# Another opening for a macaron layer: conditioning with the weights held still, spread through the first round

## What is computed

```
ada = (silu(c) @ w_ada + b_ada).reshape(B, N_MOD, D_MODEL)
xn = _modulate(_rms(x, g_ffn1), ada[:, 0], ada[:, 1])
x = x + 0.5 * ada[:, 2][:, None] * _swiglu(xn, w_ffn1_gate, w_ffn1_up, w_ffn1_down)
xn = _modulate(_rms(x, g_mix), ada[:, 3], ada[:, 4])
m, new_buf, h_last, v_state = _mixer(xn, ...)
x = x + ada[:, 5][:, None] * m
xn = _modulate(_rms(x, g_ffn2), ada[:, 6], ada[:, 7])
x = x + 0.5 * ada[:, 8][:, None] * _swiglu(xn, w_ffn2_gate, w_ffn2_up, w_ffn2_down)
```

## Time and profile before

| what | us |
| --- | --- |
| median of 3 runs | 2510.47 (2510.26 to 2513.07) |
| profiled execution | 2516.07 |
| span in its trace | 2514.3 |
| TensorE busy | 2411.8 (96%) |
| VectorE busy | 1672.5 (67%) |
| ScalarE busy | 1053.6 (42%) |
| GpSimd busy | 148.2 (6%) |

### The profile page before, as it was taken

One profiled execution on the slowest core, in us unless ns is written; L12 is line 12 of the kernel. 1 busy time (PEld: TensorE's weight loads), 2 busy tenths in 40 slices (PEclk: granted clock), 3 DMA queues, 4 the chain that ended last, 5 costly groups with the idle time before them and its releaser, 6 DMA issues.

```text
span 2514.3 us, 31914 instructions
## 1 busy us (share of the span) xinstructions
PE 2411.8 (96%) x11469; PEld 2030.0 (81%) x11469; DVE 1672.5 (67%) x2660; ACT 1053.6 (42%) x1825; POOL 148.2 (6%) x186
## 2 busy tenths in 40 slices
PE   7889999999999999999999999988999999999997
PEld 3567777777788877999999999986777788878886
DVE  4976767766666685666666666469677667656666
ACT  3454444444333353433344434135444444433334
POOL 3000000000000000000111110000000000000000
PEclk9999999999999999999999999989999999999998
DMA  9244554455976333312222123413544543497642
GB/s 359 72 159 151 176 176 150 151 177 184 346 263 226 134 126 104 127 54 63 63 63 61 56 59 98 152 55 117 175 149 151 174 147 123 151 353 278 226 134 78
DMA packets 245521, 381.03 MB, mean 152 GB/s; under 512 B 16658, under 2 KB 158154, under 8 KB 243991
## 3 DMA queue, kind: packets, MB, share of 16 engines
q1 hardware_dynamic: 232702, 345.15, 39.6%
q0 software_dynamic: 10240, 33.56, 4.9%
q10 hardware_dynamic: 2456, 0.75, 0.1%
HBM read 262.93 MB, written 116.47 MB: 151 GB/s over the span
## 4 chain that ended last, share of the span: by engine, by line
PE 71%; DVE 15%; DMA 5%; issue 4%; ACT 3%; SPq 1%; DVEq 0%; ACTq 0%
PE bank L512 21%; PE bank L513 20%; PE bank L514 20%; DMA h_dram<-stage_lo 3%; DVE u_lo L604 3%; PE bank L2800 2%; PE bank L2802 2%; PE bank L2803 2%; DMA wraw<-in_w_ffn_down 1%; DVE stage_lo L1932 1%; DVE wraw L631 1%; DVE ada_lo L1947 1%; PE bank L2818 1%; DVE h L1940 1%; DVE x L2110 1%
## 5 line engine op out<-in xcount | busy, mean ns | idle before, releaser
L604 DVE TENSOR_TENSOR u_lo<-wraw,u_hi 128x512 fp32r<-128x512 f32 (+2 forms) x532 | 317.4, 618 | 285.6 <-ACT u_hi L598 282.8
L512 PE MATMUL bank<-ops,u_hi 128*128 128x512 f32 x1232 | 488.5, 397 | 13.5 <-ACT g L1201 10.5
L513 PE MATMUL bank<-ops,u_hi 128*128 128x512 f32 x1232 | 485.3, 394 | 0.0
L514 PE MATMUL bank<-ops,u_lo 128*128 128x512 f32 x1232 | 484.2, 393 | 0.0
L598 ACT ACTIVATE u_hi<-wraw 128x512 fp32r<-128x512 f32 (+2 forms) x532 | 289.2, 567 | 267.3 <-PE bank L514 167.6
L512 PE MATMUL bank<-xn_hi,w_hi 128*128 128x384 f32 x1104 | 370.1, 335 | 6.2 <-ACT ww L1606 2.0
L514 PE MATMUL bank<-xn_hi,w_lo 128*128 128x384 f32 x1104 | 368.8, 334 | 0.0
L513 PE MATMUL bank<-xn_lo,w_hi 128*128 128x384 f32 x1104 | 368.8, 334 | 0.0
L512 PEld LDWEIGHTS bank<-ops,u_hi 128*128 128x128 f32 x1232 | 234.3, 190 | 77.4 <-ACT g L1201 11.3
L514 PEld LDWEIGHTS bank<-ops,u_lo 128*128 128x128 f32 x1232 | 233.8, 190 | 50.8
L513 PEld LDWEIGHTS bank<-ops,u_hi 128*128 128x128 f32 x1232 | 234.4, 190 | 49.1
(11 more groups left out here) (321 smaller groups left out, 4257.3 us busy)
## 6 DMA issues: line engine op xcount, KB each, us to landing
h_dram<-stage_hi SPq DMA_DIRECT2D x154, 256.0 KB, 2.4
h_dram<-stage_lo SPq DMA_DIRECT2D x154, 256.0 KB, 2.7
ada_raw<-in_w_ada POOLq DMA_DIRECT2D x96, 256.0 KB, 3.0
raw<-in_w_in SPq DMA_DIRECT2D x48, 512.0 KB, 4.7
wraw<-in_w_ffn_gate SPq DMA_DIRECT2D x44, 512.0 KB, 3.9
wraw<-in_w_ffn_up SPq DMA_DIRECT2D x44, 512.0 KB, 4.9
wraw<-in_w_ffn_down SPq DMA_DIRECT2D x48, 384.0 KB, 4.7
x<-x_dram SPq DMA_DIRECT2D x6, 2304.0 KB, 12.0
```

The lines of the kernel that those rows point to most:

```text
L512: nc.tensor.matmul(out, hi, mov_hi, start=first, stop=False, skip_group_check=True)
L513: nc.tensor.matmul(out, hi, mov_lo, start=False, stop=False, skip_group_check=True)
L514: return nc.tensor.matmul(out, lo, mov_hi, start=False, stop=last, skip_group_check=True)
L604: nc.vector.tensor_tensor(unit(u_lo, f, g, u, n), unit_source(u, n), unit(u_hi, f, g, u, n).bitcast(F32), ALU.subtract).then_inc(u_lo_read ...
```

## The change

**The conditioning products.** In `first_half` the sides are exchanged: blocks of 128x128 of the conditioning weights are stationary and the 9 columns of `cT` move, 32 matmuls a half. The result comes out turned, so the row copies (`first_rows`) and their transposes (`first_turn`) go, and VectorE adds the bias from the bank.

```diff
-FIRST_HALVES = [(v, half) for v in (SCALE1, SHIFT1, GATE1) for half in range(2)]
+FIRST_HALVES = [(SCALE1, 0), (SHIFT1, 0), (SCALE1, 1), (SHIFT1, 1), (GATE1, 0), (GATE1, 1)]
+FIRST_BANKS = (7, 6, 7, 2, 7, 7)
...
-                for k in range(KT):
-                    last = nc.tensor.matmul(bank[(3, 4, 3, 4, 7, 2)[n]][0:NSEQ, :], cT[:, k, 0:NSEQ], w_ada_sb[:, n, k, :],
-                                            start=k == 0, stop=k == KT - 1)
+                for b in range(4):
+                    o = b * NSEQ
+                    for k in range(KT):
+                        last = nc.tensor.matmul(bank[FIRST_BANKS[n]][:, o:o + NSEQ], w_ada_sb[:, n, k, b * P:(b + 1) * P],
+                                                cT[:, k, 0:NSEQ], start=k == 0, stop=k == KT - 1,
+                                                skip_group_check=True)
```

```diff
-            pe.wait_ge(rows_copied, 2)
+            pe.wait_ge(rows_copied, 1)
+            x_turn(2)
+            first_half(0)
             pe.wait_ge(x_in, 2 * NT)
-            first_half(0)
+            for c in range(3):
+                spread(0, c)
             first_half(1)
...
+                    prompt(0, A11[1], O_B11, X[1], True, False,
+                           between=(lambda: spread(2, 1)) if f == 1 else None)
+                    if f == 0:
+                        first_half(2)
+                        pe.wait_ge(xs_lo_ready, 1)
+                    else:
+                        pe.wait_ge(xs_lo_ready, 3)
                     samples_in(0, 0)
                     if f == 0:
-                        first_turn(4)
-                        first_turn(5)
-                        pe.wait_ge(ada_ready, 6)
+                        first_half(3)
...
                     prompt(0, S2[1], O_T2, X[1], False, False)
+                    if f == 0:
+                        first_half(4)
                     pe.wait_ge(snapped, snaps(f, 0, 3))
                     prompt(0, S3[0], O_T3, X[0], False, False, True)
                     pe.wait_ge(snapped, snaps(f, 0, 4))
                     prompt(0, S3[1], O_T3, X[1], False, False)
+                    if f == 0:
+                        first_half(5)
```

```diff
+            def row_squares(lo, hi):
+                for t in range(lo, hi):
+                    act.wait_ge(x_loaded[t // 3], 32 if t >= 6 else 16)
+                    if t > 1:
+                        act.wait_ge(sumsq_mm, t - 1)
+                    nc.scalar.activation(spent[:, t % 2, :], xrow[:, t, :], ACT.Square, accum_out=nrst[:, t:t + 1])\
+                      .then_inc(sumsq_mm, 1)
```

```diff
-            sp.wait_ge(x_loaded[1], 16)
             ada_half(0)
             ada_half(1)
-            first_weights(0)
+            weights(0, 0, 0, 0)
+            weights(0, 0, 1, 0)
+            sp.wait_ge(x_in, 8)
+            spill(slice(0, KH), x_spilled, slice(0, PH))
             ada_half(2)
             ada_half(3)
...
+            weights(0, 0, 0, 1)
+            weights(0, 0, 1, 1)
+            sp.wait_ge(x_spilled, 16)
+            spill(slice(KH, KT), x_spilled, slice(0, PH))
             sp.wait_ge(rg_loaded, 64)
...
+            sp.wait_ge(x_in, 2 * NT)
+            spill(slice(0, KH), x_spilled_late, slice(PH, TOK))
+            sp.wait_ge(sumsq_mm, 9)
+            ada_half(4)
+            sp.wait_ge(x_spilled_late, 16)
+            spill(slice(KH, KT), x_spilled_late, slice(PH, TOK))
```

```diff
             def sample_operand(f):
...
-                    samples_modulated(0, xs, xs, xs)
-                for k in range(KH):
-                    op_scale(f, k, 1)
+                    for k in range(KH):
+                        op_scale(f, k, 1)
                 dve.wait_ge(samples_act, FACTORS_MADE["hi", f])
...
+                if f == 1:
+                    for k in range(KH):
+                        op_scale(f, k, 1)
```

```diff
-                for o in range(2):
-                    slot_ = wslot(U_OUT + o)
-                    rows = slice(k * P, (k + 1) * P)
-                    for c in range(NCH):
+                rows = slice(k * P, (k + 1) * P)
+                for c in range(NCH):
+                    for o in range(2):
+                        slot_ = wslot(U_OUT + o)
...
-            last.then_inc(out_mm, 6)
+                        if k == KT - 1:
+                            last.then_inc(out_mm, 1)
```

More of the change, by code:

```diff
@@ L114 @@
                                (1, 4, True), (1, 6, True)]
-SQUARES = ([(c, k, False) for c in range(2) for k in range(KT)],
+SQUARES = ([],
            FFN1_SQUARES,
@@ L150, in added, with squares_done, summed_squares, sample_steps @@
 def added(i, pos):
-    return sum(is_added(j, q) for j in range(i) for q in range(NSQ)) + sum(is_added(i, q) for q in range(pos))
+    return sum(is_added(j, q) for j in range(1, i) for q in range(NSQ)) + sum(is_added(i, q) for q in range(pos))
+def squares_done(i, pos):
+    return NSQ * (i - 1) + pos + 1
+def summed_squares(i, c):
+    return (4, 8, 9)[c] if i == 0 else 9 + 3 * (i - 1) + RANK[i][c]
+def sample_steps(i):
+    return 3 * i + 3 if i > 0 else 0
 def ring_use(i, pos):
@@ L529, in made @@
     def made(f, g, u):
+        if f == 0 and isinstance(g, int) and g == 0:
+            return u + 1
         return g * 16 + (f * ALL * 16 + MADE[u] + 1)
@@ L1168, in first_units @@
             def first_units(f):
-                for u in EARLY:
+                for u in (EARLY if f == 1 else range(4)):
                     unit_hi(act, f, 0, u)
@@ L1175, in op_hi @@
                 v_shift = norm_scales(i)[0]
[L1176 removed]
+                if f == 0 and o in (O_B11, O_B21):
+                    act.wait_ge(ada_ready, 2 if o == O_B11 else 4)
+                elif f == 0 and o == O_T3:
                     act.wait_ge(ada_mm, 5)
@@ L1542, in _ @@
                     act.dma_start(rg_sb[64 * h:64 * h + 64, :, g, 64 * h:64 * h + 64], src).then_inc(rg_loaded, 16)
[L1544 to L1555 removed]
+            for c in range(3):
+                factor_copy(0, c)
             first_units(0)
@@ L2775, in units_ready, with prompt @@
                     pe.wait_ge(u_lo_ready, made(f, g, u))
-                def prompt(g, u, o, out, first, last_, staged=False):
+                def prompt(g, u, o, out, first, last_, staged=False, between=None):
                     units_ready(g, u)
@@ L2786, in prompt @@
                                        first and k == 0, last_ and k == KH - 1)
+                        if between is not None and k == 1:
+                            between()
                     last.then_inc(ffn_mm, 1)
```

351 lines of the change are left out of this document (153 added, 198 removed).

## The result

The changed kernel takes 2536.26 us (median of 4 runs, 2532.91 to 2539.12) against 2510.36 us before: a ratio of 1.0099, with a 95% interval of 1.0087 to 1.0112. The forecast was 2520, with a range up to 2529. The direction was right, the size was not: 25.9 us instead of 9.5. The profiled execution took 2532.91 us. With the six further runs of the first experiment (median 2535.12) and 29 of the kernel before beside them (median 2511.64, single executions from 2505.47 to 2518.86) the difference is 23.5 us. The two profiled executions lie only 17 us apart, since that of before was a slow one of its kind (2516.07) and that of after a quick one.

A forecast was written before the change was run, and what follows sets the result against it. TensorE, busy 96% of the span, was taken as the bound, with the opening read at VectorE's first join. Opening +17.0, FFN2 -6.8 and output projection -0.9 gave +9.3 us over the 2510.47 median: 2520 us, range 2497 to 2529.

The forecast's parts named there:

- The forecast's first step: Conditioning products: narrow passes halve the clock without a TensorE gap, a pass going from 0.106 to 0.204 us.
- rival 1: Conditioning products: the clock holds through narrow passes, 6.8 us a half, join at 121.4, time 2495 us; chance 0.22.
- The queue: Opening: late transfers make VectorE wait up to 5 us more, 2525 to 2530; chance 0.12 together with more halves at half clock.
- The waits behind halves 4 and 5: Round 0: half 4 holds ScalarE and VectorE by overwriting the place of T3's operand; TensorE then idles 3.6 us.
- the price of half 0: Start of the opening: 10.3 us from 23.19, the clock falling 3 us in; FFN1 then starts at 50.0.
- when S2 starts: Round 0 of FFN1: S2 follows T2's first low tile at 102.0 us; its 24 products end at 107.5.
- nothing between the opening and FFN2: After TensorE's wait on ada_lo at 161.57 us: no gap that matters, so no term for later rounds of FFN1.
- nothing changes between the join and the wait on ada_lo: VectorE from 129.53 to 161.57 us: same work before and after, its only long pause 3.75 us for stage-buffer stores.
- what the other edits give back: FFN2's reordered spread and sample split move its join by -6.8 us; the output projection's bank-by-bank finish gives -0.9.
- The exchange of B22 and T4: ScalarE in FFN2: B22's high parts go ahead of T4's, which costs VectorE 0.8 us.
- more halves at half clock: Conditioning halves: more than one at half clock from its start, 2.8 us each, 2526 to 2530; chance 0.12 together with The queue.

The follow-up runs named there:

- the first experiment: The changed kernel run again unaltered: median 2535.12 us (2531.86 to 2538.29), ratio 1.0096 to the kernel before.
- the second trace: Trace of the changed kernel run again unaltered; its first join stands at 154.85 us, its median time is 2535.12 us.

## Why the prediction was wrong

**What was right.** The forecast's first step, that the narrow passes let the clock fall though TensorE has no gap, and that a pass then costs 0.21 us, holds: in halves 2 to 5 the clock was at 1.00 at the start or soon after it and fell at 67.3, 81.0, 118.5 and 142.4 us, inside unbroken rows of passes. The run with 126 columns shows it as the cause: the same loads and places, 25.3 us earlier at the join. The page of the Trainium skill ("TensorE: Matmul & The Clock Gate", "HAM oscillation — how this bites in real kernels") names idle gaps as what brings the clock down. The runs show both: the gap of 4.53 us behind which a product took 0.76, and unbroken rows of 64 narrow passes at 0.50. By the gap rule alone the clock would have held through the halves, as rival 1 had it; it did not. And where it did hold for the most part, with 126 columns, the time was 2507 and not rival 1's 2495: FFN1 began at 43.00 instead of 39, and that sum had the second and third faults below too. The queue was no limit, and no wait for weights stands on the path. The waits behind halves 4 and 5 came as worked out (TensorE idle 3.90 us, forecast 3.6).

**The step that failed first: the price of half 0.** I took 10.3 us, for a half that starts at full clock. It took 13.82 in the trace of after and 12.3 in the second trace (24.13 to the first spread at 36.38). FFN1 began at 54.30 instead of 50.0. What stands ahead of half 0 is a pause of 2.55 us and short transposes, and I had treated it as work that keeps the clock up; in the trace of before the clock had stayed at 1.00 over both. The windows of after (TensorE's busy time and records, granted clock, DMA share, GB/s) show that the first fall isn't the passes':

```profile
22.00:23.00 1.00, 0.00 (x0) 0.98 1.00 371
23.00:24.00 1.00, 0.91 (x5) 0.50 1.04 381
```

The clock is at 0.50 from 22.95 us, in the pause, 0.14 us ahead of the first pass. With 126 columns it fell in the pause too, at 23.7. It can happen with wide products as well: with the opening of before and T4 first it fell at 24.7, 0.9 us into the products behind a pause of 3.31 us, and they took 15.59 us in place of 13.89:

```profile
23.76 15.59 PE L2676 MATMUL bank<-w_ada_sb,cT 128*9 128x512 f32 x32 [3.31 <-DVE x L1717]
```

But in these two the clock was back at 27.1 and 28.1. With nine columns it came back only at 60.5, behind both halves and 14 products of FFN1. So the pause can start the low stretch, and the narrow passes keep it. The sum had the second for half 0, but not the first.

**The step that failed second: when S2 starts.** The sum let S2 start with T2's first low tile. VectorE's own part of it was exact: from half 3's end, 87.95, to that tile at 106.7 it took 18.8 us, forecast 18.7. But TensorE was not free. The sample products ahead of S1 need unit 11, whose low part was ready at 100.0, and behind it stand 36 products: 4.1 us of samples, slow from 101.5 on, and 11.2 for S1 and S2. Half 4 began at 115.45. Half 3 had ended 4.7 us later than forecast, S2 ended 8.0 later; so 3.3 us are this step's.

The halves behind them were near 10.3 (9.50, 10.55, 10.84 and 9.86). Together with S3 at 8.1 instead of 7.3 this makes the join 155.2 instead of 146.5: 8.7 us, 4.3 by FFN1's start, 3.3 by S2, the rest in A11, S3 and behind it.

**The step that failed third: nothing between the opening and FFN2.** I had said that behind the wait on ada_lo TensorE goes on without a gap that matters, and had put the later rounds of FFN1 at nothing. After is 23.55 us late at the last stage buffer of round 0 and 27.95 late at 1509 us of before, so 4.4 us are lost in between. Most of it is lost at two places of one later round; the first of them in VectorE's timeline, before and then after:

```profile
359.57 0.69 DVE L1932 TENSOR_TENSOR stage_lo<-g,stage_hi 128x512 fp32r<-128x512 f32 x1 [2.47 <-ACT stage_hi L1209]
```

```profile
385.23 0.69 DVE L1959 TENSOR_TENSOR stage_lo<-g,stage_hi 128x512 fp32r<-128x512 f32 x1 [4.34 <-ACT stage_hi L1236]
```

Eight microseconds later VectorE waits 2.18 us for the high part of a unit, where it had waited 0.61. This is no scatter: in all nine traces with the changed opening the first wait is 4.0 to 4.5 us, and in the two with the opening of before it is 2.5 and 2.6. From the last stage buffer of round 0 to 1509 us of before the nine lose 1.4 to 9.2 us, the two 0.0 and 0.7. Why the stage buffers come free later there no run tests. In the other direction I had said that nothing changes between the join and the wait on ada_lo: the moved bank copies take the stage buffer's wait from 3.75 to 2.35 there, and 2.1 us come back.

**The term that was too large: what the other edits give back.** Forecast were -6.8 and -0.9. In the traces they come nearly in full: from 27.9 to 26.8 over the output projection, from 26.8 to 21.1 at FFN2's join and to 19.5 at its last stage buffer. But I had read FFN2's waits in an execution in which the clock was at 0.50 for 10.2 us behind its sums (1674.5 to 1684.7); in both traces of after and in both runs with the opening of before and the other edits it was 6.8. By medians the edits without the exchange of sides give 4.8, about 5 behind the first stage buffer, in place of 7.7. The exchange of B22 and T4 I priced at 0.8; it costs 2.1 at the join with early halves, 1.9 with the opening of before, each without the part that stands ahead of it, and 1.8 and 2.4 by medians. A wait that is read in one trace is a price only if the clock beside it is read too.

From the traces, then, it is 25.7 - 2.1 + 4.4 - 1.1 - 7.3 - 2.7 = +16.9, the difference of the two spans; the -2.7 fall behind FFN2's first round, where the two kernels do the same, and I leave them open. The medians are 23.5 apart, since the two executions lie 4.4 over and 2.2 under theirs. With the price of the other edits by medians the sum is 23.6 + 4.4 - 5 = 23.0.

**The range.** Its upper end, 2529, was put together from a late queue and more halves at half clock, 2.8 us each. The first came to nothing and the second happened once (half 0). That TensorE waits for a unit which VectorE makes later than its operands was in no case, and neither was a loss in the later rounds.

## What to carry to other kernels

Where few columns move against full weight loads, look at the granted clock before you count passes: if it falls in that stretch, stream the same operand several times over into spare bank columns. Here 126 columns in place of 9 made a pass cost 0.114 us instead of 0.216, and the kernel 27.8 us faster. Put such work where TensorE waits anyway, and not in front of the stretch that an overlaid buffer holds back; that was worth another 16.7 us, and the kernel with both and T4's parts first runs in 2488.95 us, 0.9903 of before (0.9885 to 0.9921). When a schedule is worked out, write down for every product the last of all its inputs, not only the one that the edit moves.

## What the runs showed of the hardware

- With 36 moving columns the granted clock was 0.57 from 20 to 60 us, hardly more than with 9 (0.54), and with 126 it was 0.91. I had expected 36 to lie nearer the middle.
- At full clock a pass with a full 128x128 float32 load took 0.106 us with one column, 0.113 with 36 and 0.114 with 126, and 0.12 with 128 in the sums (1.95 / 16): up to there the moved columns cost almost nothing.
- The fall can begin in a pause and be kept up by what follows: it came at 22.95 us with nine columns and 23.7 with 126, both in the pause ahead of half 0, and ended at 60.5 in the one and at 27.1 in the other.
- A pause of 4.5 us of TensorE was followed by products of 0.76 us where 0.47 is usual (79.53 with 126 columns). With the pause filled the granted clock stayed at 1.00 from 60 to 100 us:

```profile
60.00:100.00 40.00, 38.08 (x263) 1.00 0.40 146
```
